# Shared expert by seven quarter products, with sums in PSUM and four slot scatters under way

## The reference

```python
h = layer_norm(DN_ALPHA * h + mix, ln1_g, ln1_b)
# routing: sigmoid scores of 64 experts, 4 of 8 groups, top 8 per token, weights normalised
scores = sigmoid(xt @ router_w); sel = scores + router_b
...
def swiglu(x, w_gu, w_down):
    gate, up = split(x @ w_gu, 2)          # w_gu 1024 x 512, w_down 256 x 1024
    return (silu(gate) * up) @ w_down
ffn = routed_experts(...) + swiglu(h, sh_w_gu, sh_w_down)
ple = sigmoid(h @ ple_w_g + ple_b_g) * (p @ ple_w_e)
h = layer_norm(DN_ALPHA * h + ffn + ple, ln2_g, ln2_b)
```

## Time and profile before

| | |
|---|---|
| timed runs (3) | median 2316.85 us, 2315.64 to 2322.55 |
| profiled execution | 2325.7 us, span 2323.9 us |
| busy PE, DVE, ACT, POOL | 97%, 50%, 20%, 33% |
| mean granted clock of PE | 0.986 |
| output projection ends, down products start, gate stage starts | 1234.4, 1310.9, 1338.4 us |
| experts start, last expert's down products end | 1453.8, 2263.5 us |

### The profile page before, as it was taken

How to read it: one execution, slowest core, us unless ns; L and a number is a source line. 1 busy time by engine, 2 the same in 40 slices (tenths; PEclk the granted TensorE clock), 3 DMA queues, 4 the chain that set the end, 5 groups by cost and what they waited for, 6 DMA issues and landing times.

```text
span 2323.9 us, 26832 instructions
## 1 busy us (share of the span) xinstructions
PE 2261.9 (97%) x9664; PEld 1331.3 (57%) x9664; DVE 1162.8 (50%) x2027; ACT 465.3 (20%) x779; POOL 758.0 (33%) x756
## 2 busy tenths in 40 slices
PE   9999999999999999999999999999999999999995
PEld 5784554445894444444445477665666656565653
DVE  7543887887646445555764755222222222223225
ACT  3001125655331110111012100111111111111113
POOL 1000110003520000000000356567676675766652
PEclk9999999999999999999999999999999999999998
DMA  8111001122012111010605013999999998999975
GB/s 311 61 57 53 26 11 60 55 73 74 3 44 75 55 64 55 30 52 28 227 37 208 23 55 118 343 354 363 331 345 321 331 350 286 350 313 351 328 250 180
DMA packets 142581, 386.12 MB, mean 166 GB/s; under 512 B 22700, under 2 KB 51616, under 8 KB 141426
## 3 DMA queue, kind: packets, MB, share of 16 engines
q1 hardware_dynamic: 110258, 307.49, 35.8%
q0 software_dynamic: 31152, 70.09, 11.9%
q10 hardware_dynamic: 1040, 6.83, 0.7%
HBM read 328.86 MB, written 66.58 MB: 170 GB/s over the span
## 4 chain that ended last, share of the span: by engine, by line
PE 90%; DVE 4%; issue 2%; DMA 1%; ACT 1%; POOL 0%; another core or an unknown queue 0%; POOLq 0%; SPq 0%; DVEq 0%; ACTq 0%
PE banks L2678 13%; PE banks L1916 12%; PE banks L2686 9%; PE banks L2723 9%; PE banks L465 6%; PE banks L1928 6%; PE banks L1139 5%; PE banks L2520 4%; PE banks L2626 3%; PE banks L512 3%; PE banks L2505 2%; PE banks L340 2%; PE banks L1151 2%; PE banks L2614 1%; PE banks L2701 1%
## 5 line engine op out<-in xcount | busy, mean ns | idle before, releaser
L2678 PE MATMUL banks<-arena 128*128 128x136 f32 (+8 forms) x2240 | 325.5, 305 | 22.6 <-issue 22.4
L3405 POOL DMA_INDIRECT arena<-hp_scratch,arena x300 | 305.2, 1017 | 101.4 <-issue 90.7
L2678 PEld LDWEIGHTS banks<-arena 128*128 128x128 f32 x2240 | 315.2, 196 | 32.4 <-issue 32.4
L1916 PE MATMUL banks<-arena 128*128 128x512 f32 x672 | 290.5, 592 | 0.0
L2686 PE MATMUL banks<-arena 128*128 128x512 f32 (+1 forms) x528 | 237.6, 592 | 0.3 <-ACT arena L2863 0.3
L1916 PEld LDWEIGHTS banks<-arena 128*128 128x128 f32 x672 | 127.2, 189 | 160.1 <-issue 160.1
L2723 PE MATMUL banks<-arena 128*128 128x512 f32 x464 | 207.1, 598 | 5.3 <-DVE arena L3226 5.3
L3421 POOL DMA_INDIRECT acc_scratch<-arena x97 | 150.6, 1553 | 151.0 <-DVE arena L3299 61.5
L286 POOL TENSOR_SCALAR arena<-arena 128x1 f32<-128x1 f32 x16 | 4.9, 306 | 562.7 <-DVE arena L277 562.7
L3226 DVE STREAM_TRANSPOSE arena<-arena 128x1024 f32<-128x1024 f32 (+3 forms) x97 | 96.2, 999 | 158.4 <-DMA arena<-gt_scratch,arena 149.2
L2686 PEld LDWEIGHTS banks<-arena 128*128 128x128 f32 (+1 forms) x528 | 97.3, 188 | 111.3 <-issue 110.0
(11 more groups left out here) (480 smaller groups left out, 2990.4 us busy)
## 6 DMA issues: line engine op xcount, KB each, us to landing
arena<-in_exp_w_gu SPq DMA_DIRECT2D x64, 2048.0 KB
arena<-in_exp_w_down SPq DMA_DIRECT2D x64, 1024.0 KB
arena<-in_w_in SPq DMA_DIRECT2D x22, 1024.0 KB, 5.5
arena<-in_w_in SPq DMA_DIRECT2D x5, 2048.0 KB, 7.8
arena<-in_w_branch SPq DMA_DIRECT2D x12, 512.0 KB, 6.5
arena<-in_ple_w_g SPq DMA_DIRECT2D x3, 2048.0 KB
hp_scratch<-arena SPq DMA_DIRECT2D x10, 512.0 KB, 3.1
acc_scratch<-arena SPq DMA_DIRECT2D x10, 512.0 KB, 4.5
```

What stands on the lines that cost most here:

```text
L1916: last = nc.tensor.matmul(PS[:, g % 4, :], lhs[:, k, :], rhs[:, k, :], start=(k == 0), stop=(k == 3))
L2678: last = nc.tensor.matmul(PS[:, bank + part, f * n:(f + 1) * n], weights[:, k, part * FF + f * P:part * FF + (f + 1) * P], x[:, k, 0:n], s ...
L3405: nc.gpsimd.indirect_dma_start(out=rows[0:n, :], out_offset=None, in_=table, in_offset=bass.IndirectOffsetOnAxis(ap=at, axis=0), bounds_ch ...
```

## The change

The shared expert's gate and up are computed as one product of 2 by 2 quarters, with seven quarter products instead of eight. For each f the weights are four quarters, `shared_quarter(f, c, j)`: c is gate or up, j the half of the depth. The tokens are four quarters, `shared_tokens(j, half)`. POOL makes four sums of weight quarters for each f, DVE four sums of token quarters (T1 to T4, over 384 and then 128 columns), in `base`. PE computes products 0 to 6 for both f, each of four matmuls 512 wide. Some are accumulated on another in the same bank (1, 3 and 5 on 0; 6 on 4). ACT copies the bank at four stages, and DVE adds the other bank's sum to two of the copies for each f. The Silu of the second half of the tokens stands behind the copies of turned p.

Around it: both last tiles are turned and all logits done before the second product; the mask products stand after the eighth product, the rank products after the eleventh, the row after the thirteenth. The gate weights wait for all fourteen products (`base` is taken until then), one after the other, and the bias row behind them. Their sums on DVE move to later down groups. Four slot scatters may be under way instead of two, and the slot table is turned in iteration 4 instead of 5.

```diff
-SLOTS_AT = 5
+SLOTS_AT = 4
+SCATTERS = 4
...
+            sh_sums = carve(6 * HALF, R3 + 2 * SEQ + NT * PLE).rearrange("p (f x k n) -> p f x k n", f=2, x=3, k=4)
+            sh_T = [carve(4 * HALF, base + x * 4 * HALF).rearrange("p (k s) -> p k s", k=4) for x in range(4)]
...
-                sp.dma_start(bg_row, row("ple_b_g", 0, D)).then_inc(f_bg, 16)
-                wg_v = a["ple_w_g"].rearrange("(k p) n -> p k n", p=P)
-                for j in range(2):
-                    sp.dma_start(wg[:, j, :, :], wg_v[:, :, j * HALF:(j + 1) * HALF]).then_inc(f_wg, 16)
...
+                sp.wait_ge(f_gu, 14)
+                wg_v = a["ple_w_g"].rearrange("(k p) n -> p k n", p=P)
+                for j in range(2):
+                    if j:
+                        sp.wait_ge(f_wg, 16)
+                    sp.dma_start(wg[:, j, :, :], wg_v[:, :, j * HALF:(j + 1) * HALF]).then_inc(f_wg, 16)
+                sp.dma_start(bg_row, row("ple_b_g", 0, D)).then_inc(f_bg, 16)
...
+                def shared_product(f, idx):
+                    T1, T2, T3, T4 = sh_T
+                    lhs, rhs = {0: (shared_quarter(f, 0, 0), shared_tokens(0, 0)), 1: (shared_sum(f, 2), T2),
+                                2: (shared_quarter(f, 0, 1), shared_tokens(1, 0)), 3: (shared_sum(f, 3), T3),
+                                4: (shared_sum(f, 1), T1), 5: (shared_quarter(f, 1, 1), T4),
+                                6: (shared_sum(f, 4), shared_tokens(1, 1))}[idx]
+                    bank = (4 if idx in (0, 1, 3, 5) else 6) + f
+                    for k in range(4):
+                        last = nc.tensor.matmul(PS[:, bank, :], lhs[:, k, :], rhs[:, k, :],
+                                                start=(k == 0 and idx in (0, 2, 4)), stop=(k == 3), skip_group_check=True)
...
                 last = 11 * (OPAIRS - 1)
+                turn_tile(NT - 2)
                 pe.wait_ge(f_w, 32)
                 pe.wait_ge(o_res, last + O_DONE[1])
-                shared_gate_up(0, 0)
-                turn_tile(NT - 2)
-                logits(NT - 4)
+                shared_product(0, 0)
+                turn_tile(NT - 1)
+                for t in range(NT - 4, NT):
+                    logits(t)
                 pe.wait_ge(o_res, last + O_DONE[3])
-                shared_gate_up(0, 1)
-                turn_tile(NT - 1)
-                logits(NT - 3)
-                logits(NT - 2)
+                shared_product(1, 0)
                 pe.wait_ge(o_res, last + O_DONE[5])
-                shared_gate_up(1, 0)
-                logits(NT - 1)
+                shared_product(0, 2)
                 pe.wait_ge(o_res, last + O_DONE[6])
-                shared_gate_up(1, 1)
-                pe.wait_ge(f_sl, 1)
-                shared_gate_up(2, 0)
-                pe.wait_ge(f_up, 1)
-                shared_gate_up(2, 1)
+                shared_product(1, 2)
+                pe.wait_ge(o_t, OUT_T + 6)
+                for f in range(2):
+                    pe.wait_ge(o_u, OUT_U + f + 1)
+                    pe.wait_ge(o_s, OUT_S + 4 * f + 2)
+                    shared_product(f, 1)
+                pe.wait_ge(o_t, OUT_T + 7)
+                pe.wait_ge(o_s, OUT_S + 3)
+                pe.wait_ge(o_u, OUT_U + 3)
+                shared_product(0, 3)
+
+                pe.wait_ge(o_s, OUT_S + 7)
+                pe.wait_ge(o_u, OUT_U + 4)
+                shared_product(1, 3)
...
-                pe.wait_ge(f_sl, 2)
-                shared_gate_up(3, 0)
+                for f in range(2):
+                    pe.wait_ge(o_res, OUT_R + f + 1)
+                    shared_product(f, 4)
+
+                pe.wait_ge(o_t, OUT_T + 8)
+                pe.wait_ge(o_u, OUT_U + 5)
+                shared_product(0, 5)
...
-                pe.wait_ge(f_up, 2)
-                shared_gate_up(3, 1)
+                pe.wait_ge(o_u, OUT_U + 6)
+                shared_product(1, 5)
+                pe.wait_ge(o_res, OUT_R + 3)
+                pe.wait_ge(o_s, OUT_S + 4)
+                shared_product(0, 6)
...
+                pe.wait_ge(o_res, OUT_R + 4)
+                pe.wait_ge(o_s, OUT_S + 8)
+                shared_product(1, 6)
...
+                    if q % NT == 0:
+                        pe.wait_ge(f_hid, 2 + 2 * (q // NT))
                     if q >= 2:
                         pe.wait_ge(f_acc, q - 1)
+                    else:
+                        pe.wait_ge(o_res, OUT_R + 5 + q)
...
+                shared_copied(1, 0, shared_slice(0, 0), 4, o_u)
                 act.wait_ge(e_lg, NT)
                 nc.scalar.activation(sc, PS[:, 2, :], ACT.Sigmoid).then_inc(e_sc, 1)
-                for q in range(4):
-                    half, f = q // 2, q % 2
-                    act.wait_ge(f_gu, 2 * q + 1)
-                    nc.scalar.activation(hid[:, f, half * HALF:(half + 1) * HALF], PS[:, 4 + 2 * (q % 2), :], ACT.Silu).then_inc(f_sl, 1)
-                    act.wait_ge(f_gu, 2 * q + 2)
-                    if q >= 2:
-                        act.wait_ge(f_hid, q - 1)
-                    nc.scalar.activation(up[q % 2], PS[:, 5 + 2 * (q % 2), :], ACT.Copy).then_inc(f_up, 1)
+                shared_copied(2, 1, shared_slice(1, 0), 4, o_u)
+                for f in range(2):
+                    shared_copied(5 + f, f, second_gate[f], 4, o_u)
+                for f in range(2):
+                    shared_silu(1 + f, shared_slice(f, 0))
+                for f in range(2):
+                    shared_copied(7 + f, f, shared_slice(f, 1), 4, o_u)
+                for f in range(2):
+                    shared_copied(11 + f, f, up[f], 4, f_up)
...
+                for f in range(2):
+                    shared_silu(5 + f, second_gate[f])
...
+                def shared_token_sums(tiles, lo, n):
+                    T1, T2, T3, T4 = (x[:, :, lo:lo + n] for x in sh_T)
+                    first, second = ([shared_tokens(j, half)[:, :, lo:lo + n] for j in range(2)] for half in range(2))
+                    at = OUT_T + (4 if lo else 0)
+                    v.wait_ge(o_hT, 2 * tiles)
+                    nc.vector.tensor_tensor(T1, second[0], first[0], ALU.subtract).then_inc(o_t, 1)
+                    v.wait_ge(o_t, at + 1)
+                    nc.vector.tensor_tensor(T2, second[1], T1, ALU.subtract).then_inc(o_t, 1)
+                    nc.vector.tensor_tensor(T3, second[1], second[0], ALU.subtract).then_inc(o_t, 1)
+                    v.wait_ge(o_t, at + 2)
+                    nc.vector.tensor_tensor(T4, first[1], T2, ALU.subtract).then_inc(o_t, 1)
+
+                def shared_added(f, product, copied, dst):
+                    v.wait_ge(o_u, OUT_U + copied)
+                    v.wait_ge(f_gu, product)
+                    nc.vector.tensor_tensor(dst, dst, PS[:, 6 + f, :], ALU.add).then_inc(o_res, 1)
+
+                v.wait_ge(o_job, 7 * OPAIRS)
+                shared_token_sums(NT - 1, 0, 3 * P)
+                shared_token_sums(NT, 3 * P, P)
...
+                    shared_added(f, 3 + f, 1 + f, hid[:, f, 0:HALF])
...
+                    shared_added(f, 9 + f, 5 + f, hid[:, f, HALF:SEQ])
...
+                shared_added(0, 13, 3, second_gate[0])
...
+                shared_added(1, 14, 4, second_gate[1])
...
-                    if q in (2, 4, 8, 10):
-                        gate_weight_sum(0, {2: 1, 4: 2, 8: 3, 10: 4}[q])
-                    if q == 6:
-                        gate_token_sum(0, 1)
-                        gate_token_sum(0, 2)
+                    if q in (8, 10, 12, 14):
+                        gate_weight_sum(0, {8: 1, 10: 2, 12: 3, 14: 4}[q])
+                    if q in (4, 6):
+                        gate_token_sum(0, q // 2 - 1)
...
+                    S1, S2, S3, S4 = (shared_sum(f, x) for x in (1, 2, 3, 4))
+                    at = OUT_S + 4 * f
+                    nc.gpsimd.tensor_tensor(S1, shared_quarter(f, 1, 0), shared_quarter(f, 1, 1), ALU.add).then_inc(o_s, 1)
+                    pool.wait_ge(o_s, at + 1)
+                    nc.gpsimd.tensor_tensor(S2, S1, shared_quarter(f, 0, 0), ALU.subtract).then_inc(o_s, 1)
+                    nc.gpsimd.tensor_tensor(S3, shared_quarter(f, 0, 0), shared_quarter(f, 1, 0), ALU.subtract).then_inc(o_s, 1)
+                    pool.wait_ge(o_s, at + 2)
+                    nc.gpsimd.tensor_tensor(S4, shared_quarter(f, 0, 1), S2, ALU.subtract).then_inc(o_s, 1)
...
-                        if i >= 2:
-                            pool.wait_ge(e_slots[i % 2], 16 * (i // 2))
+                        if i >= SCATTERS:
+                            pool.wait_ge(e_slots[i % SCATTERS], 16 * (i // SCATTERS))
                         nc.gpsimd.indirect_dma_start(
                             out=slot_d, out_offset=bass.IndirectOffsetOnAxis(ap=pos_i[:, i:i + 1], axis=0),
-                            in_=tok_id[:, t:t + 1], in_offset=None).then_inc(e_slots[i % 2], 16)
+                            in_=tok_id[:, t:t + 1], in_offset=None).then_inc(e_slots[i % SCATTERS], 16)
```

(19 more changed lines are left out.)

32 lines of the change are left out of this document (21 added, 11 removed).

## The result

The changed kernel takes 2350.14 us (median of 4 runs, 2347.62 to 2352.11) against 2318.59 for the kernel before (4 runs, 2315.64 to 2322.55): ratio 1.0148, interval 1.0128 to 1.0167. It is slower by 1.5%; 2303.0, faster by 0.6%, was forecast. The profiled execution took 2352.1 us, span 2350.3, mean clock 0.981.

A forecast was written before the change was run, and what follows sets the result against it. TensorE (PE), busy 97% of 2323.9 us, was taken as the bound: 7.1 us saved in the products, 1.0 lost at the slots, 7.8 saved at the experts' start, 13.9 off the 2316.85 median, giving 2303.0; range 2298 to 2313.

The forecast's parts named there:

- sum 2: Slot scatters: four under way cut 108.35 us to 87.7 or 90; slots ready at 1403 to 1407.
- The slower rival: Slot scatters: completions come in order, four under way bring nothing; PE stands 16.1 us, total 2321.4; chance 0.07.
- the 1.0 charged for the slots: Gate loop, iteration 4: PE reaches the turned slots about when they are ready; 1.0 us of waiting charged.
- sum 1: PE's queue from tile 3's logits to the first down product: 63.4 us instead of 70.53, 7.1 us earlier.
- the cover: Token sums on VectorE before the scores: done at about 1252.5, second needed by PE at 1262.9, so no cost.
- only the seven products count: Whole kernel: the experts' start pause brings no gain; only 7.1 us less up to 1, giving 2309.8; chance 0.30.
- 2 to 3 us for loads: Slot scatters: gate weights, bias row and embedding weights arriving under the first dozen add 2 to 3 us.
- Sum 3: Start of the experts: the 5.3 us wait and 2.5 us of slow matmuls go away, 7.8 us.
- the other end of the bound: Start of the experts: if VectorE is held again, the whole gain is 6 us instead of 13.9.

The follow-up runs named there:

- experiment 1: Changed kernel with two scatters under way instead of four and the slots turned in iteration 5, as before; 2326.41 us, ratio 1.0004.
- experiment 8: Changed kernel, slots in iteration 5, second place's gathers waiting for the first's: two scatters under way 2314.81 us; four, all landed before every 12th, 2309.30 us.
- experiment 2: The kernel before with four scatters under way instead of two, nothing else changed; 2358.79 us, ratio 1.0141.
- 4: Changed kernel, four under way, all landed before every 8th scatter: 2337.92 us; before every 16th, with slots in iteration 5: 2328.85 us.
- 5: Changed kernel, slots in iteration 5, GpSimd fills instead of landing waits before every 16th scatter: one fill 2353.62 us, ten fills 2339.29 us.
- experiment 6: Changed kernel, slots in iteration 5: one fill before every second scatter, 2348.40 us; three under way plus a wait before the second place's gathers, 2345.79 us.
- experiment 3: Changed kernel with four scatters still under way but the slots turned in iteration 5, as before; 2358.61 us, ratio 1.0156.

## Why the prediction was wrong, point by point

**Failed: sum 2, "with four under way most of the 27.5 us falls away".** As arithmetic on POOL it nearly held. From the first issue (1308.51) to the end of the last (1402.00) are 93.5 us, forecast 90; 12.3 of them are waits for landings, forecast under 8. The last issue was forecast near 1398 and came at 1401.04; the slots were ready at 1407.25, forecast 1403 to 1407. What failed is the term under it that was put at nothing: that POOL's waits can go without a price on another engine. Without them PE lost 38.1 us of waits, and DVE's additions came late with it. I searched for a wait that takes the place of the one removed among semaphores and buffers; the price was paid by PE, which shares neither with the scatters. No rival had it. The slower rival, completions in order, named the right direction, but its mechanism was not what happened: the slots came 14 us before its 1421.6. The earlier trace rows held a warning: asking when PE's 33 pieces of "issue" came would have shown 29 of them at the ends of POOL's longest runs.

The size follows from the trace. The first expert was forecast at 1442.4. The gate loop started 0.8 us later than forecast, the third iteration took 43.0 us more (38.1 of waits, the other 4.9 beside a granted clock of 0.5), and the 1.0 charged for the slots wasn't used: 1442.4 + 0.8 + 43.0 - 1.0 = 1485.2, measured 1485.23.

**Held: sum 1.** From the logits of tile 3 to the down products are 64.4 us, forecast 63.4, before 70.53. PE waits 0.24 us for the mask, which comes at 1276.97 instead of 1271.8, and 0.25 us for a copy of ScalarE. The sizes of DVE's and POOL's pieces were off where they ran side by side. DVE's timeline of after:

```profile
1239.93 2.29 DVE L281 SCALAR_TENSOR_TENSOR arena<-arena 128x1024 f32<-128x1024 f32 x1 [0.46 <-POOL arena L289]
...
1244.18 2.83 DVE L3107 TENSOR_TENSOR arena<-arena 128x1536 f32<-128x1536 f32 x1
1247.04 2.53 DVE L3109 TENSOR_TENSOR arena<-arena 128x1536 f32<-128x1536 f32 x1
```

The sums of 1536 took 2.5 to 2.8 us, not 1.75, and the normalisation's product 2.29, not 1.28; POOL's 512-wide sums took up to 2.79 us, against bounds of 1.09 and an assumed 2.5. DVE was done at 1259.28 instead of 1252.5, and the cover held, though most of it was used up. The Trainium skill, "SBUF — State Buffer", section "SBUF: two separate sides", says that a VectorE operation with two SBUF inputs and a GpSimd operation that reads SBUF hold one pair of ports in turn, each for its whole length. By that rule an estimate of the upper bound is the sum of the forecast's 1.75 us (itself an estimate from the earlier trace rows) and the 1.09 us of the earlier trace rows, 2.84 us; the 2.83 measured agrees.

**Not realised: what sum 1 gives.** The rival "only the seven products count", at 2309.8, was nearest to what experiment 1 tests, and that gave 1.0004. The 6 us that PE gains end in the wait for the slots: scatters that start earlier, beside the gate weights, end no earlier. This was in the working as 2 to 3 us for loads, but only for the case of four.

**Sum 3, half right.** The late additions at the start of the experts go with the place of the gathers, as forecast: in the changed kernel, with the gathers ahead of the last iteration's end and fewer loads beside them, the first expert took 6.88 us and waited for nothing. Whether it is the traffic or the scatters just ahead of the gathers that makes the additions late is not shown. In experiment 1 they came back (6.04 us), as the other end of the bound said. With gathers of two places apart (experiment 8) part moves to the second place (3.1 and 3.7 us).

**What is shown and what isn't.** Shown: four scatters under way make the loss, alone and whole (experiment 2); waits for all landings every 8 or 12 scatters (10 to 17 us) take the stop away, every 16 most of it (4, 8); fills that lengthen a gap from 0.30 to 0.39 us, or three under way instead of four, do not (5, 6). The Trainium skill, "DMA: Bandwidth & Descriptors", Anatomy of one DMA (SWDGE path), puts the 2 us of such a transfer mostly on its receipt and says that many descriptors can be emitted before an incremental cost shows up. The pauses of 2.0 to 2.8 us in experiment 8 fit the 2 us, and GpSimd's own issues stay at 1.26 us for all 45; here the cost is TensorE's, after 15 issues or more.

Open: what in the chip holds PE and DVE up. The trace of after has no packet on the queues of instructions between 1343 and 1412 us, that of before four. But PE, which stands from 1382.92, starts again at 1409.64, before the next such packet begins (1413.4); in experiment 3 it starts again at 1401.40 and the packet comes at 1404.4. So in these stops PE didn't wait for a packet that the trace shows. And PE's 115 matmul records between the two packets around the stop are as many as elsewhere (98 to 159), so the missing packets rather follow from PE's standing. Open too: whether the rate of issues counts, and why the first 22 scatters of experiment 2 held nothing up. Not tried: the kernel before with pauses at 12 and four under way but without the products, which would say how much of the 0.27% is the products'.

## What to carry to other kernels

Before taking GpSimd's waits out of a series of indirect transfers, look at what TensorE and VectorE do in its longest uninterrupted stretches. In this kernel their work mostly gets late 18 to 26 us into one, though one of 30.1 us held nothing up. Stretches of 12 scatters (15 to 17 us) with a wait for all landings between them were safe in the gate loop. Measure each pause, since the same wait placed in the experts' gathers cost 1.5%. A step saved in front of a transfer is worth only as much as the transfer ends earlier; here 64 scatters that started 4.8 us sooner, under 4 MB of loads, ended 0.7 us later. And check in the trace that a delay put in as a test delays: the single fills of experiments 5 and 6 added 0.09 us each.

## What the runs showed of the hardware that I had not expected

- 45 indirect transfers issued one every 1.26 us stopped TensorE for 38.1 us while the DMA engines were 3% busy; the clock was at 1.2 instead of 2.4 GHz for 41.0 us, from 1371.7 to 1412.6, 3 us beyond the end of the stop.
- In such a stretch the chain shows pauses of VectorE of 15.22 us (experiment 2) and 19.17 us (the fills of experiment 6) with no releaser named.
- The same kernel with gaps of 2.1 to 3.4 us every 16 scatters took 2323.75 us in one run and 2353.93 in another.
- A run of 22 such transfers over 30.1 us (experiment 2) left TensorE without a wait.
